# Retention layer on one Trainium2 core: gate projections of two heads in one product, chunk products in three fp32r passes, one state update in eight left out

## The chip, the cores and the metric

The kernel runs on one core of a Trainium2 chip. The metric is the device time of one execution in microseconds (us), taken as the median of several. A core has a matrix engine (TensorE, PE in the profile, with its weight loads as PEld), a vector engine (VectorE, DVE), a scalar engine (ScalarE, ACT), GpSimd (POOL) and a sync engine (SyncE, SP) that here only waits and issues transfers (SPq rows). Each engine runs its own instruction list in order; they meet only in semaphores.

## The reference, cut to what matters

The whole program is a retention layer, a latent attention layer and a gated linear attention layer with its MLP, on 1024 tokens of width 1024. Only the retention layer is changed. It computes, for 8 heads with 128-wide queries and keys, 256-wide values and a 256-wide gate:

```python
proj = rmsnorm(x, g_pre) @ w_in                      # 1024 x 6144
q, k, v, gate = split(proj)                          # per head 128, 128, 256, 256
q = rope(q);  k = rope(k) * RET_QK_DIM ** -0.5
# per head, with a state R (128 x 256) carried over chunks of tokens
o = (q @ k.T * decay) @ v + (q @ R) * xi
R = R * g_c + (k * zeta).T @ v
o = groupnorm(o) * gn_gain
y = (silu(gate) * o) @ w_out
x = x + rmsnorm(y, g_post)
```

The kernel takes chunks of 128 tokens. The state after a head's last chunk is read by nothing.

## The kernel before, in words

**Precision.** The large products are done in fp32r, a format in which a product is one pass of the array. A matrix is split into an upper part (a rounded copy, made by ACT) and a lower part (the rest, made by DVE), and a product is three passes: lower by upper, upper by lower, upper by upper. The small products of a chunk (scores, scores by values, queries by state, keys by values) are plain fp32, which the trace shows as two records for each matmul.

**Loops.** The retention stage is 64 steps: head h = 0 to 7 outside, token tile t = 0 to 7 (128 tokens) inside, s = 8h + t. The first head and the last are written out, the ones between stand in a loop. A head's weights (8 row tiles kt of 128 x 768: q, k, v and gate columns) are loaded with 768 KB for two row tiles, then split by `w_upper` (ACT) and `w_lower` (DVE), one row tile in each step of the head before. There are two slots for split weights (`inh`, `inl`) and two for raw ones (`inraw`).

**One step on each engine**, in program order:
- PE (`step`): `project` of tile s into q, k, v (24 matmuls of 512 columns); the two transposes of q and k of s-1; `attend(s-2)` (the products `ra_o_ps` by scores, `ra_o_ps` by state, `ra_k_ps`); `project` of the gate of s (24 of 256 columns); `scores(s-1)`.
- ACT: `w_upper` of the next head; copy of the transposed q, k of s-1; copy of q, k, v of s out of PSUM; copy of the output of s-2; `silu` of the gate of s.
- DVE: `w_lower`; `norm_and_gate(s-3)`, which gives the finished tile and counts `G_done`; `carry_state(s-2)`; `moments(s-2)`; `decay_scores(s-1)`, which gives `sT` and counts `sT_done`.
- POOL: rotation of q, k of s (six operations), the decayed keys `kz`, then `deviation(s-2)`.
- SP (`head`): for even t, `load_raw` of row tiles t and t+1 of the next head; then `store(s-3)`, which waits for `G_done` of s-3 and issues the store of the gated tile to DRAM. Whatever stands behind this wait is issued only after it.

**After the last head** the gated tiles come back from DRAM, are transposed, and are multiplied by the 16 row tiles of `w_out` (512 KB each, split by `row_upper` on ACT and `row_lower` on DVE, through raw places given by `row_place`). The first three row tiles are split inside the retention block, and PE does the first four half-products (`multiply`) between the last two `attend`.

Of the kernel before, what the change touches and what calls it, by code (L numbers as in the profile page):

```python
# [17 lines left out]
F32 = mybir.dt.float32  # L18
# [70 lines left out]
def retention_columns(w):  # L89

    w = w.reshape(KT, P, -1)
    parts = [w[:, :, 0:DM].reshape(KT, P, RET_HEADS, RQK), w[:, :, DM:2 * DM].reshape(KT, P, RET_HEADS, RQK),
             w[:, :, 2 * DM:2 * DM + RET_W].reshape(KT, P, RET_HEADS, RV),
             w[:, :, 2 * DM + RET_W:].reshape(KT, P, RET_HEADS, RV)]
    return np.ascontiguousarray(np.concatenate(parts, axis=3).transpose(2, 1, 0, 3))
# [63 lines left out]
def retention_and_latents(nc, place, x, x_cols, gain_in, w_in, gated, w, gain, g_post, x_next, g_kv, g_pre, w_lat, w_gate, g_lat,  # L159
# [8 lines left out]
    with ExitStack() as ctx:  # L168
# [10 lines left out]
        WC = QKV + RV  # L179
        tokh = place("ra_xh", [P, KT, SEQ], F32R, 0)  # L180
        tokl = place("ra_xl", [P, KT, SEQ], F32R, 32 * KB)
        inh = place("ra_wh", [P, 2, KT, WC], F32R, 64 * KB)
        opening = place("ra_opening", [P, 2 * KT * WC], F32, 112 * KB)
        inl = place("ra_wl", [P, 2, KT, WC], F32R, 112 * KB)
        inraw = place("ra_raw", [P, 2, 2, WC], F32, 160 * KB)
        rcos = place("ra_cos", [P, NT, RQK // 2], F32, 172 * KB)
        rsin = place("ra_sin", [P, NT, RQK // 2], F32, 174 * KB)
        decay = place("ra_decay", [P, RET_HEADS, P], F32, 176 * KB)
        qkv = place("ra_qkv", [P, 2, QKV], F32, 180 * KB)
        rot = place("ra_rot", [P, 2, 2, RQK], F32, 184 * KB)  # L190
        rtmp = place("ra_rtmp", [P, 2, RQK], F32, 186 * KB)
        kz = place("ra_kz", [P, 2, RQK], F32, 187 * KB)
        qkT = place("ra_qkT", [P, 2, 2, P], F32, 188 * KB)
        sT = place("ra_sT", [P, P], F32, 190 * KB)
        R = place("ra_R", [P, RV], F32, 190 * KB + 512)
        sg = place("ra_sg", [P, 4, RV], F32, 191 * KB + 512)
        oS = place("ra_oS", [P, 2, RV], F32, 195 * KB + 512)
        SMALL = 197 * KB + 512
# [9 lines left out]
        def cols(t):  # L208

            return staging[:, t % 2, :].rearrange("p (k n) -> p k n", k=KT)  # L210

        def rows(t):

            at = 2 * KT * WC - (2 - t % 2) * DM
            return opening[:, at:at + DM]

        def first_raw(kt):

            return inraw[:, kt // 2, kt % 2, :] if kt < 4 else opening[:, (KT + kt - 4) * WC:(KT + kt - 3) * WC]
# [7 lines left out]
        ROW_AT = [80] + [8 * i for i in range(8)] + [88, 96, 136, 144, 152, 104, 168]  # L227
# [7 lines left out]
        row3 = place("wa_row3", [P, DM], F32, 168 * KB)  # L235
# [7 lines left out]
        LH_FREE, LL_FREE, XH_FREE, XL_FREE = 4, 7, (9, 11), (12, 14)  # L243
# [21 lines left out]
        with ExitStack() as second:  # L265
# [11 lines left out]
        first_in = [sem(f"ra_first_in{i}") for i in range(4)]  # L277
        inraw_in = [sem("ra_raw_in0"), sem("ra_raw_in1")]
        g_out = [sem(f"ra_g_out{i}") for i in range(4)]
        (xss_done, xrms_part, xrms_done, tokh_done, tokl_done, inh_done, inl_done, qkv_mm, qkv_copied,  # L280
         rot_part, rot_done, kz_done, qkT_mm, qkT_copied, s_mm, sT_done, attend_mm, R_done, o_copied, gate_mm,
         silu_done, bn_part, mv_done, rstd_part, rstd_done, norm_part, G_done) = (sem("ra_" + n) for n in (
            "ss_done xrms_part xrms_done tokh_done tokl_done inh_done inl_done qkv_mm qkv_copied "
            "rot_part rot_done kz_done qkT_mm qkT_copied s_mm sT_done attend_mm R_done o_copied gate_mm "
            "silu_done bn_part mv_done rstd_part rstd_done norm_part G_done").split())
        LAST = RET_HEADS * NT
        N_CON = 6
# [4 lines left out]
        row3_in = sem("wa_row3_in")  # L292
# [19 lines left out]
        gin1 = xin[:, :, :].rearrange("p a n -> p (a n)")[:, 0:KW * P].rearrange("p (k n) -> p k n", n=P)  # L312
        EARLY_A = {1: (0, 0), 2: (0, 1), 3: (0, 2), 5: (0, 3), 6: (1, 1), 7: (1, 3)}
        EARLY_B = {5: (1, 0), 6: (1, 2)}
# [5 lines left out]
        def row_place(kt):  # L320

            if kt == 3:
                return row3[:, :], row3_in, 16
            if kt in (6, 7, 10, 11, 14, 15):
                return y[:, kt % 2, :], y_row_in[kt % 2], 16 * ((kt - 2) // 4)
            if kt < 2:
                return staging[:, kt, :], w_arrived[kt], 16
            slot, nth = {2: (0, 2), 4: (1, 2), 5: (0, 3), 8: (1, 3), 9: (0, 4), 12: (1, 4), 13: (0, 5)}[kt]
            return staging[:, slot, :], w_arrived[slot], 16 * nth
# [33 lines left out]
        def _(sp):  # L363
            def load_cols(t):
                if t >= 2:
                    sp.wait_ge(tokl_done, t - 1)
                sp.dma_start(staging[:, t % 2, :], x_cols[t, :, :]).then_inc(cols_in[t % 2], 16)

            def load_rows(t):
                if t >= 2:  # L370
                    sp.wait_ge(xss_done, t - 1)
                sp.dma_start(rows(t), x[t * P:(t + 1) * P, :]).then_inc(rows_in[t % 2], 16)

            def load_first(kt):
                to = (KT + kt - 4) * WC
                dst = inraw[:, kt // 2, :, :] if kt < 4 else opening[:, to:to + 2 * WC].rearrange("p (k n) -> p k n", k=2)
                sp.dma_start(dst, w_in[0, :, kt:kt + 2, :]).then_inc(first_in[kt // 2], 16)

            def load_raw(h, kt):
                slot = kt // 2 % 2  # L380
                sp.dma_start(inraw[:, slot, :, :], w_in[ds(h, 1), :, kt:kt + 2, :].rearrange("a p k n -> p (a k) n"))\
                  .then_inc(inraw_in[slot], 16)
# [3041 lines left out]
```

## Time and profile before

| | us |
|---|---|
| median of 3 runs | 2610.97 (2609.92 to 2613.78) |
| the profiled execution | 2608.52 |
| its span in the trace | 2606.7 |
| PE busy | 2556.7 (98%) |
| DVE busy | 1146.5 (44%) |
| ACT busy | 864.9 (33%) |
| POOL busy | 418.7 (16%) |

Read it so: PE is busy nearly all the time over the whole program, so what counts is how much PE work there is and where PE waits. The retention stage lies from 0 to about 666 us; the rest is the same in both kernels. Busy time of matmuls overlaps (they are pipelined), so the cost of one is read from the distance between the starts of two, not from its duration.

### The profile page before, as it was taken

Reading aid. Unit: us, or ns where it says so; the run is one execution under the profiler, and the core shown is the slowest. Engines: PE = TensorE matmul, PEld = TensorE weight load, DVE = VectorE, ACT = ScalarE, POOL = GpSimd, SP = SyncE. Lnnn points to the kernel's source line nnn. Section 1 sums busy time; section 2 is a strip of 40 time slices with the busy share of each in tenths; the row PEclk is TensorE's granted clock in tenths of the full one; section 3 lists DMA queues with packets and bytes.
Section 4 is the critical chain, followed back from the end, with each engine's and each line's share of the span. In section 5 each row is a group of like instructions: output and inputs, shape, how many; then the busy total and the mean of one; then the engine's idle time right before and its main releaser. Section 6 shows DMA issues by size and latency. Waiting matters only on the chain.

```text
span 2606.7 us, 35858 instructions
## 1 busy us (share of the span) xinstructions
PE 2556.7 (98%) x13176; PEld 2180.0 (84%) x13176; DVE 1146.5 (44%) x2235; ACT 864.9 (33%) x1584; POOL 418.7 (16%) x892
## 2 busy tenths in 40 slices
PE   8999999999999999999999999999999999999999
PEld 7888888888887987788878888888888888888887
DVE  4333333322512521477765777666343343334334
ACT  5322222222312422555444545343331122112212
POOL 4443434343100312200001011101000000000000
PEclk9999999999999999999999999999999999999999
DMA  6211111120523322121243111122331120112111
GB/s 238 76 50 50 48 61 49 50 73 27 202 73 111 98 77 71 30 59 58 70 156 130 60 44 44 46 67 94 126 130 49 49 64 32 48 48 64 32 49 73
DMA packets 71877, 194.21 MB, mean 75 GB/s; under 512 B 8160, under 2 KB 28000, under 8 KB 71008
## 3 DMA queue, kind: packets, MB, share of 16 engines
q1 hardware_dynamic: 71776, 192.85, 22.5%
q8 instruction: 65, 1.06, 0.2%
q14 instruction: 36, 0.29, 0.0%
HBM read 152.45 MB, written 36.18 MB: 72 GB/s over the span
## 4 chain that ended last, share of the span: by engine, by line
PE 53%; DVE 4%; issue 2%; ACT 2%; DMA 0%; ACTq 0%; DVEq 0%; POOL 0%; POOLq 0%
PE wc_g_ps L3197 13%; PE wc_y_ps L3213 13%; PE gl_vr_ps L2334 7%; PE gl_j_ps L2293 3%; PE wb_y_ps L2664 3%; PE wc_y_ps L2946 3%; PE gl_l_ps L2360 2%; DVE at_nmax L1577 1%; PE at_v_ps L1652 1%; DVE gate_lower L1584 1%; PE at_v_ps L1653 1%; PE at_v_ps L1654 1%; PE at_j_ps L1652 1%; PE gl_o_ps L2345 1%; PE gl_k_ps L2348 1%
## 5 line engine op out<-in xcount | busy, mean ns | idle before, releaser
L1068 PE MATMUL ra_qkv_ps<-ra_wh,ra_xl 128*128 (+1 forms) x512 | 207.0, 404 | 11.5 <-DVE ra_wl L903 9.2
L1068 PE MATMUL ra_qkv_ps<-ra_wh,ra_xh 128*128 (+1 forms) x512 | 201.3, 393 | 0.0
L1068 PE MATMUL ra_qkv_ps<-ra_wl,ra_xh 128*128 (+1 forms) x512 | 200.8, 392 | 0.0
L3197 PE MATMUL wc_g_ps<-x_upper,ff_w1l 128*128 128x512 f32 x512 | 199.3, 389 | 0.0
L3197 PE MATMUL wc_g_ps<-x_upper,ff_w1h 128*128 128x512 f32 x512 | 199.2, 389 | 0.0
L3213 PE MATMUL wc_y_ps<-ff_w2h,ff_hl 128*128 128x512 f32 x512 | 199.2, 389 | 0.0
L3213 PE MATMUL wc_y_ps<-ff_w2l,ff_hh 128*128 128x512 f32 x512 | 199.2, 389 | 0.0
L3197 PE MATMUL wc_g_ps<-x_lower,ff_w1h 128*128 128x512 f32 x512 | 199.2, 389 | 0.0
L3213 PE MATMUL wc_y_ps<-ff_w2h,ff_hh 128*128 128x512 f32 x512 | 199.2, 389 | 0.0
L3151 DVE TENSOR_TENSOR ff_acc<-wc_y_ps,ff_acc 128x1024 f32<-128x1024 f32 x63 | 77.1, 1225 | 210.9 <-PE wc_y_ps L3213 210.9
L3076 ACT ACTIVATE ff_relu<-wc_g_ps 128x512 f32<-128x512 f32 x64 | 38.3, 598 | 378.1 <-PE wc_g_ps L3197 378.1
L1068 PE MATMUL ra_gate_ps<-ra_wh,ra_xl 128*128 (+1 forms) x512 | 155.7, 304 | 0.0
L1068 PE MATMUL ra_gate_ps<-ra_wh,ra_xh 128*128 (+1 forms) x512 | 144.7, 283 | 0.0
L1068 PE MATMUL ra_gate_ps<-ra_wl,ra_xh 128*128 (+1 forms) x512 | 144.6, 282 | 0.0
L3137 DVE SCALAR_TENSOR_TENSOR wc_g_ps<-wc_g_ps,ff_relu 128x512 f32<-128x512 f32 x64 | 44.8, 700 | 178.8 <-ACT ff_relu L3076 178.8
L1068 PEld LDWEIGHTS ra_qkv_ps<-ra_wh,ra_xl 128*128 128x128 f32 x512 | 97.1, 190 | 30.0 <-issue 11.7
L570 ACT ACTIVATE ra_qkT<-ra_T_ps 128x256 f32<-128x256 f32 x63 | 24.1, 383 | 282.1 <-PE ra_T_ps L1078 282.1
L1068 PEld LDWEIGHTS ra_qkv_ps<-ra_wh,ra_xh 128*128 128x128 f32 x512 | 97.0, 189 | 21.4
L3213 PEld LDWEIGHTS wc_y_ps<-ff_w2l,ff_hh 128*128 128x128 f32 x512 | 96.1, 188 | 19.9
L3213 PEld LDWEIGHTS wc_y_ps<-ff_w2h,ff_hl 128*128 128x128 f32 x512 | 96.1, 188 | 19.9
L3197 PEld LDWEIGHTS wc_g_ps<-x_lower,ff_w1h 128*128 128x128 f32 x512 | 96.1, 188 | 19.9
L3197 PEld LDWEIGHTS wc_g_ps<-x_upper,ff_w1h 128*128 128x128 f32 x512 | 96.1, 188 | 19.9
(409 smaller groups left out, 6442.4 us busy)
## 6 DMA issues: line engine op xcount, KB each, us to landing
staging<-in_w_ff SPq DMA_DIRECT2D x64, 512.0 KB, 3.8
ra_raw<-in_w_in_a SPq DMA_DIRECT2D x30, 768.0 KB, 4.6
gated_a<-ra_sg SPq DMA_DIRECT2D x64, 128.0 KB, 1.9
staging<-in_w_vr_c SPq DMA_DIRECT2D x16, 512.0 KB, 4.2
wa_gin<-gated_a SPq DMA_DIRECT2D x6, 1024.0 KB, 4.9
staging<-in_w_out_a SPq DMA_DIRECT2D x9, 512.0 KB, 4.1
staging<-in_x_cols SPq DMA_DIRECT2D x8, 512.0 KB, 5.1
ra_opening<-in_x SPq DMA_DIRECT2D x8, 512.0 KB, 7.6
```

Source lines behind the costliest of these rows:

```text
L1068: last = pe.matmul(out, a[:, kt, t * P:(t + 1) * P], b[:, ds(slot, 1), kt, at:at + n].rearrange("p a n -> p (a n)"), start=(kt == 0 and i ...
L1652: pe.matmul(out, al, bh, start=start, stop=False)
L2293: last = pe.matmul(out, w[:, r, cols], xx[:, r, at], start=(r == 0 and i == 0), stop=(r == KT - 1 and i == 2))
L2334: last = pe.matmul(vr_ps[t % 2][:, :], xx[:, r, t * P:(t + 1) * P], w[:, r, :], start=(r == 0 and i == 0), stop=(r == KT - 1 and i == 2))
L2360: last = pe.matmul(l_ps[:, level * (P // 2):(level + 1) * (P // 2)].rearrange("p (g n) -> p g n", n=n), lv_main[c][:, level, at], lv_main[ ...
L2664: last = pe.matmul(y_ps[t % 2][:, c, :], a[t % 2][:, kt, :], b[kt][:, c * HALF:(c + 1) * HALF], start=(kt == 0 and i == 0), stop=(kt == KW ...
L2946: last = pe.matmul(y_ps[t % 2][:, c, :], a[t % 2][:, kt, :], b[kt][:, c * HALF:(c + 1) * HALF], start=(kt == 0 and i == 0), stop=(kt == KW ...
L3076: act.activation(relu[:, :], f_ps[j % 2][:, :], ACT.Relu).then_inc(relu_done, 1)
L3137: dve.scalar_tensor_tensor(f_ps[j % 2][:, :], f_ps[j % 2][:, :], 0.0, relu[:, :], ALU.max, ALU.mult).then_inc(sq_done, 1)
L3151: dve.tensor_tensor(acc[t][:, :], y_ps[t % 2][:, :, :].rearrange("p a n -> p (a n)"), acc[t][:, :], ALU.add).then_inc(y_added, 1)
L3197: last = pe.matmul(f_ps[j % 2][:, :], a[kt // 2][:, kt % 2, f * P:(f + 1) * P], b[:, kt, half * HALF:(half + 1) * HALF], start=(kt == 0 an ...
L3213: last = pe.matmul(y_ps[t % 2][:, n, :], a[:, f, t * P:(t + 1) * P], b[f][:, n * HALF:(n + 1) * HALF], start=(f == 0 and i == 0), stop=(f ...
```

## The change

- `retention_columns` now lays the weights out as a wide array for each pair of heads (q, k, v of the even head, the gates of both heads: 1024 columns) and a narrow one (q, k, v of the odd head: 512 columns). PE's gate product is done in the even head alone, 512 columns wide, for both; `silu` writes the odd head's half into `kept`, which lies in `staging`.
- There is one slot each for wide and narrow split weights. The next pair's wide weights are loaded one row tile (512 KB) in each step of the odd head and split there (`wide_upper`, `wide_lower`); the narrow ones two row tiles (512 KB) in every other step of the even head.
- The three chunk products run in three fp32r passes (`three`). So the scores, the transposed queries, the state, the decayed keys and the values are split: upper parts by ACT (the keys' by POOL's own product), lower parts by DVE (`scores_lower`, `queries_lower`, `state_lower`, `keys_lower`, `values_lower`).
- `scores` moves from the end of step s+1 to the middle of `project` in step s+2, two steps behind.
- For t = 7 the product `ra_k_ps` and the state update are left out.
- The first row tiles of `w_out` go other ways: 0, 1, 3, 4 through `inraw`; 2 and 5 through `staging`, which holds `kept` until the last tiles are stored; row 5 is loaded only after the last store has landed. Four row tiles are split inside the block.

```diff
-            def head(h, first, more):
+            def load_wide(pair, kt):
+                sp.wait_ge(inl_done, splits(pair, kt - 2))
+                sp.dma_start(inraw[:, kt % 2, :], w_wide[ds(pair, 1), :, kt, :].rearrange("a p n -> p (a n)"))\
+                  .then_inc(inraw_in[kt % 2], 16)
...
+            def odd_head(pair):
+                h = 2 * pair + 1
                 for t in range(NT):
-                    if more and t % 2 == 0:
-                        sp.wait_ge(inl_done, t + 2 if first and t < 4 else KT * h + KT + t - 2)
-                        load_raw(h + 1, t)
...
+                    load_wide(pair + 1, t)
+                    if t == 3:
+                        sp.wait_ge(sT_part, NT * h)
+                        load_decay(h + 1, 0)
+                    store_third_last(h, True, t)
+
+            def even_head(pair):
+                h = 2 * pair
+                for t in range(NT):
+                    if t % 2 == 0:
+                        load_narrow(pair, t // 2)
+                    if t == 3:
+                        sp.wait_ge(sT_part, NT * h)
+                        load_decay(h + 1, 1)
+                    store_third_last(h, False, t)
```

ACT, first for the order in a step, then for the first head and the odd heads:

```diff
+            def step(s, h, t, older, middle=lambda: None):
+
+                if older >= 2:
+                    scores_upper(s - 2)
+                middle()
+                act.wait_ge(qkv_mm, s + 1)
+                if older < 4:
+                    act.wait_ge(xrms_done, t + 1)
+                act.activation(qk[:, t % 2, :], qkv_ps[t % 2][:, 0:2 * RQK], ACT.Copy, scale=xrms[:, 1, t:t + 1]).then_inc(qkv_copied, 1)
                 if older >= 1:
+                    transposed(s - 1, (t - 1) % NT)
                 if older >= 2:
                     act.wait_ge(attend_mm, s - 1)
+                act.activation(vh[:, t % 2, :], qkv_ps[t % 2][:, 2 * RQK:QKV], ACT.Copy, scale=xrms[:, 1, t:t + 1]).then_inc(vh_done, 1)
                 if older >= 2:
+                    output(s - 2, h if t >= 2 else h - 1, (t - 2) % NT, older >= 4)
...
             for t in range(NT):
-                step(t, 0, t, t)
-                silu(t, 0, t, t)
+                if t == NT - 2:
+                    act.wait_ge(tokl_done, NT)
+                if t >= NT - 2:
+                    for i in (2 * t - 2 * NT + 4, 2 * t - 2 * NT + 5):
+                        narrow_upper(0, i)
+                step(t, 0, t, min(t, 3))
+                silu(0, t, True)
                 if t + 2 < NT:
                     square_x(t + 2)
                     x_upper(t + 2)
-                w_upper(1, 1, t)
...
+            def odd_head(pair):
+                h = 2 * pair + 1
                 for t in range(NT):
+                    if t == 0:
+                        act.wait_ge(gate_mm, NT * pair + NT)
+                    wide_upper(pair + 1, t)
                     step(h * NT + t, h, t, 4)
```

DVE:

```diff
+            def step(s, pair, odd, t, older, middle=lambda: None):
...
+                if older >= 2:
+                    decay_scores(s - 2, *head_of(2), (t - 2) % NT)
+                if older >= 1:
+                    keys_lower(number(1), (t - 1) % NT)
+                if older >= 2:
+                    scores_lower(s - 2)
+                middle()
+                if older >= 3:
+                    norm_and_gate(s - 3, *head_of(3), (t - 3) % NT)
+                if older >= 1:
+                    queries_lower(s - 1, (t - 1) % NT)
+                if older >= 2:
+                    carry_state(s - 2, number(2), (t - 2) % NT)
+                values_lower(s, t)
+                if older >= 2:
+                    moments(s - 2, (t - 2) % NT)
+                    state_lower(number(2), (t - 2) % NT)
...
+            def odd_head(pair):
                 for t in range(NT):
+                    wide_lower(pair + 1, t)
+                    step((2 * pair + 1) * NT + t, pair, True, t, 3)
```

PE:

```diff
+            def three(out, high, low, start, stop):
+
+                (ah, bh), (al, bl) = high, low
+                pe.matmul(out, al, bh, start=start, stop=False)
+                pe.matmul(out, ah, bl, start=False, stop=False)
+                return pe.matmul(out, ah, bh, start=False, stop=stop)
...
+            def step(s, h, t, weights, older, pair=None, between=lambda: None, middle=lambda: None):
                 if older >= 2:
+                    pe.wait_ge(vl_done, s - 1)
+                out, as_they_come = qkv_ps[t % 2][:, :], None if older else 0
+                project(out, t, weights, 0, range(KT // 2), as_they_come)
+                if older >= 2:
+                    scores(s - 2)
+                middle()
+                project(out, t, weights, 0, range(KT // 2, KT), as_they_come).then_inc(qkv_mm, 1)
                 if older >= 1:
                     transpose_qk(s - 1, (t - 1) % NT, older >= 2)
                 if older >= 2:
+                    attend(s - 2, h if t >= 2 else h - 1, (t - 2) % NT, older >= 3)
                 between()
+                if pair is not None:
+                    if older:
+                        pe.wait_ge(silu_done, NT * pair + t)
+                    project(gate_ps[:, :], t, weights, QKV, range(KT), None if older else KT).then_inc(gate_mm, 1)
```

## Rows read from the trace of the kernel before

**Rows 1.** The waits of PE, 0 to 900 us: total, times, longest.

```profile
PE ra_qkv_ps L1068 <- DVE ra_wl L903: 9.2, 1, 9.2
...
PE ra_qkv_ps L1068 <- DVE ra_wl L864: 2.4, 1, 2.4
PE wa_y_ps L346 <- DVE wa_wl L339: 1.7, 1, 1.7
```

**Rows 2.** Timeline of PE over one step: start us, us, engine, line, operands, count.

```profile
299.73 0.47 PE L1068 MATMUL ra_gate_ps<-ra_wh,ra_xl 128*128 x1
...
300.15 0.28 PE L1068 MATMUL ra_gate_ps<-ra_wh,ra_xh 128*128 x1
...
302.78 0.39 PE L1098 MATMUL ra_s_ps<-ra_qkT 128*128 128x128 f32 x2
...
303.70 0.40 PE L1068 MATMUL ra_qkv_ps<-ra_wh,ra_xl 128*128 x1
...
308.25 0.39 PE L1068 MATMUL ra_qkv_ps<-ra_wh,ra_xh 128*128 x1
308.49 0.38 PE L1078 MATMUL ra_T_ps<-ident,ra_rot 128*128 128x128 f32 x2
308.70 0.60 PE L1089 MATMUL ra_o_ps<-ra_qkv,ra_sT 128*128 128x256 f32 x2
309.14 0.59 PE L1091 MATMUL ra_o_ps<-ra_R,ra_qkT 128*128 128x256 f32 x2
309.57 0.59 PE L1092 MATMUL ra_k_ps<-ra_qkv,ra_kz 128*128 128x256 f32 x2
309.81 0.47 PE L1068 MATMUL ra_gate_ps<-ra_wh,ra_xl 128*128 x1
```

**Rows 3.** Timeline around a store and a load, DVE and SP queue, same columns.

```profile
105.95 0.43 DVE L876 TENSOR_TENSOR ra_sg<-ra_oS,ra_sg 128x256 f32<-128x256 f32 x1
...
106.55 0.34 SPq L387 DMA_DIRECT2D gated_a<-ra_sg  x1
...
107.14 0.36 SPq L381 DMA_DIRECT2D ra_raw<-in_w_in_a  x1
```

**Rows 4.** DMA issues of 100 to 600 us: KB each, median us from issue to landing.

```profile
ra_raw<-in_w_in_a SPq DMA_DIRECT2D x23, 768.0 KB, 4.5
gated_a<-ra_sg SPq DMA_DIRECT2D x50, 128.0 KB, 1.9
```

**Rows 5.** DMA issues of 1900 to 2600 us, the same columns.

```profile
staging<-in_w_ff SPq DMA_DIRECT2D x60, 512.0 KB, 3.7
```

**Rows 6.** Groups of ACT, 0 to 700 us: busy us, mean ns of one, idle before.

```profile
L588 ACT ACTIVATE ra_sg<-ra_gate_ps,ra_rx 128x256 f32<-128x256 f32 x64 | 30.4, 475 | 109.9 <-PE ra_gate_ps L1068 109.9
...
L570 ACT ACTIVATE ra_qkT<-ra_T_ps 128x256 f32<-128x256 f32 x63 | 24.1, 383 | 282.1 <-PE ra_T_ps L1078 282.1
L335 ACT ACTIVATE wa_wh<-staging,gains 128x1024 fp32r<-128x1024 f32 x9 | 10.3, 1147 | 9.6 <-DMA staging<-in_w_out_a 9.5
```

**Rows 7.** Groups of DVE, 0 to 700 us, the same columns.

```profile
L876 DVE TENSOR_TENSOR ra_sg<-ra_oS,ra_sg 128x256 f32<-128x256 f32 x64 | 27.2, 426 | 2.2
...
L872 DVE TENSOR_SCALAR ra_oS<-ra_oS,ra_mv,ra_rstd 128x256 f32<-128x256 f32 x64 | 26.3, 411 | 28.8 <-POOL ra_rstd L784 28.8
L898 DVE TENSOR_TENSOR ra_sT<-ra_s_ps,ra_decay 128x128 f32<-128x128 f32 x64 | 18.7, 291 | 77.0 <-PE ra_s_ps L1098 77.0
...
L339 DVE SCALAR_TENSOR_TENSOR wa_wl<-staging,gains,wa_wh 128x1024 fp32r<-128x1024 f32 x9 | 11.5, 1284 | 9.4 <-ACT wa_wh L335 9.4
```

**Rows 8.** Timeline of PE from its wait at 88 us.

```profile
90.75 0.54 PE L1068 MATMUL ra_qkv_ps<-ra_wh,ra_xl 128*128 x1 [2.37 <-DVE ra_wl L864]
...
94.50 0.39 PE L1068 MATMUL ra_qkv_ps<-ra_wh,ra_xl 128*128 x1
```

**Rows 9.** Timeline of the SP queue at the end of the stage.

```profile
670.09 0.34 SPq L387 DMA_DIRECT2D gated_a<-ra_sg  x1
...
674.15 0.33 SPq L461 DMA_DIRECT2D wa_gin<-gated_a  x1
```

More of the change, by code:

```diff
@@ L91, in retention_columns @@
     w = w.reshape(KT, P, -1)
[L92 to L95, printed above, removed]
+    qk = [w[:, :, i * DM:(i + 1) * DM].reshape(KT, P, RET_HEADS, RQK) for i in range(2)]
+    v, gate = (w[:, :, 2 * DM + i * RET_W:2 * DM + (i + 1) * RET_W].reshape(KT, P, RET_HEADS, RV) for i in range(2))
+    own = np.concatenate(qk + [v], axis=3)
+    wide = np.concatenate([own[:, :, 0::2], gate[:, :, 0::2], gate[:, :, 1::2]], axis=3)
+    lay = lambda part: np.ascontiguousarray(part.transpose(2, 1, 0, 3))
+    return lay(wide), lay(own[:, :, 1::2])
 def wait_alone(eng):
@@ L208, in cols, with first_raw, gated_tile, states @@
         def cols(t):
[L210 to L219, printed above, removed]
+            src = staging if t < 2 else late_cols
+            return src[:, t % 2, :].rearrange("p (k n) -> p k n", k=KT)
+        def first_raw(kt, half):
+            return first_raws[kt // 2][:, kt % 2, half * HALF:(half + 1) * HALF]
+        def gated_tile(odd, t):
+            return kept[:, t, :] if odd else sg[:, t % 4, :]
+        def states(h, t):
+            return (NT - 1) * h + t
+        WIDES, NARROWS = KT, KT // 2
+        PIECES = WIDES + NARROWS
+        def splits(pair, j):
+            return PIECES * pair + KT + j + 1
         KW = RET_W // P
@@ L565, in step, with first_upper, wide_upper @@
-            def step(s, h, t, older):
-                hp = h if t >= 2 else h - 1
+            def first_upper(kt, half):
+                act.wait_ge(first_in[half][kt // 2], 16)
+                act.activation(wide[0][:, kt, half * HALF:(half + 1) * HALF], first_raw(kt, half), ACT.Copy,
+                               scale=gain_in[:, kt:kt + 1]).then_inc(inh_done, 1)
+            def wide_upper(pair, kt):
+                act.wait_ge(inraw_in[kt % 2], 16 * (PIECES // 2 * pair + kt // 2 - KT // 2 + 1))
+                act.activation(wide[0][:, kt, :], inraw[:, kt % 2, :], ACT.Copy, scale=gain_in[:, kt:kt + 1]).then_inc(inh_done, 1)
@@ new lines, in narrow_upper, with scores_upper @@
+            def narrow_upper(pair, i):
+                act.wait_ge(inraw_in[i % 2], 16 * (PIECES // 2 * pair + i // 2 + 1))
+                for kt in (2 * i, 2 * i + 1):
+                    last = act.activation(narrow[0][:, kt, :], inraw[:, i % 2, kt % 2 * NARROW:(kt % 2 + 1) * NARROW],
+                                          ACT.Copy, scale=gain_in[:, kt:kt + 1])
+                last.then_inc(inh_done, 1)
+            def scores_upper(s):
+                act.wait_ge(sT_part, s + 1)
+                act.activation(sTh[:, :], sT[:, :], ACT.Copy).then_inc(sTh_done, 1)
@@ L1120, in _ @@
                     pe.wait_ge(ident_in, 16)
[L1121 removed]
+                step(t, 0, t, wide, t, 0)
             def transpose_first(tile, q):
```

528 lines of the change are left out of this document (298 added, 230 removed).

## The prediction

> **What bounds the kernel now.** I read the waits of PE first [rows 1]: over the whole retention stage PE waits 9.2 us at the start, 2.4 us once, and 1.7 us once in the product that follows. Between these it never waits for another engine, so the stage is the sum of its matmuls. The timeline of one step gives their prices [rows 2]. A step, from gate product to gate product, is 309.81 - 299.73 = 10.08 us. A 512-column pass takes (308.25 - 303.70)/20 = 0.2275 us, a 256-column pass (302.78 - 300.15)/22 = 0.1195 us. The three fp32 products start 0.44 and 0.43 us apart, and I take 0.43 for the third. So PE has no slack, and every other engine has. The question is what slack is left when a step of PE gets short. For that I read the queue around a store and a load [rows 3], what a load takes to land [rows 4, 5], and what an element-wise operation costs on ACT and DVE [rows 6, 7].
>
> **Part 1: gates of two heads in one product.** Before, two heads pay 48 x 0.1195 = 5.74 us for a tile's gates, after 24 x 0.2275 = 5.46 us [rows 2]: 0.28 us saved, 32 times, **-9.0 us**.
>
> **Part 2: three passes.** 3 x 0.1195 = 0.36 us in place of 0.43 to 0.44 [rows 2]. Scores by values 64 x 0.08 = 5.1, queries by state 56 x 0.07 = 3.9, keys by values 56 x 0.07 = 3.9 us: **-12.9 us**. That a pass keeps its 0.1195 us here is taken from the gate's passes; the other bound is a rival below.
>
> **Part 3: last state.** 8 x 0.43 = **-3.4 us** [rows 2].
>
> **Part 4: the new step lengths.** An even head's step becomes 10.08 - 2.87 + 5.46 - 0.22 = 12.45 us, an odd head's 10.08 - 2.87 - 0.22 = **6.99 us**. The parts add up to the same: 12.45 + 6.99 is 0.72 us under 2 x 10.08.
>
> **Part 5: what the short step uncovers.** In heads 1, 3 and 5 the wide weights are fetched and split, one row tile a step. SP's list is: load of row tile t, then the store of tile s-3, which waits for `G_done` of s-3; only then comes the load of t+1. But ACT wants t+1 ahead of everything else in step s+1, DVE splits it ahead of `decay_scores(s-1)`, and `norm_and_gate(s-2)`, which gives the next `G_done`, stands behind that on DVE. So there is a ring that goes round once a step, and the load is inside it:
>
> - end of the gating product to the issue of the load: 107.14 - 106.38 = 0.76 us [rows 3] (the store's own issue lies between);
> - issue to landing of 512 KB: 3.7 us, the median of 60 loads of this size [rows 5]. From the 128 and 768 KB of this stage, 1.9 and 4.5 us, a straight line gives 3.46 [rows 4]; 4.5 is the upper bound;
> - `wide_upper`, 128x1024: 1.15 us [rows 6];
> - handing on to another engine: 0.17 us (DVE's end at 106.38 to SP's issue at 106.55 [rows 3]);
> - `wide_lower`, 128x1024: 1.28 us [rows 7];
> - `decay_scores`: 0.29 us, with its start 0.32 [rows 7];
> - handing on, `scores_upper`: 0.17 + 0.28 us. No copy of 128x128 is in the trace; it lies between nothing and the 0.38 us of 256 columns [rows 6], and I take it near the upper end;
> - handing on, `scores_lower`: 0.17 + 0.27 us, just under the 0.29 of its neighbour [rows 7];
> - `norm_and_gate`: 0.41 + 0.43 us with starts, 0.90 [rows 7].
>
> The sum is **9.17 us** against 6.99 us of PE work. PE stands in this ring too: `attend(s-2)` waits for `sT_done`, so behind it `project` of the next step waits. Each round costs 2.18 us. Step 0 of an odd head is free of it, since its row tile was loaded during the long even step. In step 1 the load is issued 6.7 us after the last gate product and the scores are ready at 14.3, where PE would come at 12.9: 1.4 us. Steps 2 to 7 cost 6 x 2.18 = 13.1 us. Step 0 of the next even head meets the narrow load in the same ring. Its two 512-column splits take 1.28 us on ACT and 1.42 us on DVE (between the 256- and 1024-column prices of rows 6 and 7), so 9.44 - 6.99 = 2.45 us. Together 17.0 us for a pair, three times: **+51 us**. In the other even steps the same ring has 12.45 us and is hidden. In head 7 nothing wide is loaded. There the early work on `w_out` is two row tiles that came long before; the chain from `attend` through copy, split and scores ends about 0.4 us before PE needs it, so I cost it at nothing.
>
> The Trainium skill ("DMA: Bandwidth & Descriptors", section on the anatomy of one DMA) fits a transfer as about 2.0 us plus its bytes at 436 GB/s, which is an estimate of 3.2 us for 512 KB, for a path other than SP's. By it the forecast would be some 11 us lower; the measured 3.7 us is used. Its constant part alone would leave the ring longer than PE's step, so this rule speaks against the change as well.
>
> **Part 6: head 0.** Before, PE waited 2.37 us when head 1's last split came late, and then ran at half clock: nine passes in 94.50 - 90.75 = 3.75 us instead of 2.05 [rows 8]. After, the narrow weights are ready before the last gate product ends: **-4.1 us**. What takes its place is in step 6. ACT does `silu` twice (0.95 us [rows 6]), squares and copies the last tile (two of 128x1024, 2.3 us), then waits for `x_lower` (1.28 us on DVE) before the first `narrow_upper`, because these weights lie on the column buffer. Then come four copies of 512 columns (2.56), the last pair's split (1.42) and the scores' chain (1.21, from the ring). Counted from `attend` with PE's 6.54 us to the end of its gate product that is 17.0 us against 12.45: 4.6 us late. Step 7 is 0.6 us late, steps 2 to 5 0.2 us each: **+6 us**. In the opening, DVE's half pieces of 512 columns let PE start about 1 us sooner, and the first gate product then waits for eight more pieces. I take no change, within 2 us either way.
>
> **Part 7: the end of the stage.** Before, PE lost 1.7 us there [rows 1]. After, I follow the lists from the last `attend` but two. The state split of tile 62 stands ahead of the last scores on DVE: 1.0 us. `row_lower(2)` comes behind the last scores: 0.6. `row_lower(3)` and `row_lower(4)` stand behind the last two tiles' normalisation, which takes DVE, POOL and DVE in turn: 1.3 us each. Row tile 5 can be asked for only when the last store has landed (1.9 us, median [rows 4]; here before 4.06 us lay between that issue and the next block's first load, with other loads under way [rows 9]). It then needs 3.7 + 1.15 + 0.17 + 1.28 us while PE has one row tile of 2.7 us left: 4.8 us late, and then likely half clock, 1.7 us. Together 10.7, less the old 1.7: **+9 us**.
>
> **Part 8: clock.** A wait of 1.7 us [rows 1] left the passes behind it at full rate, one of 2.37 us halved it [rows 8]. In the odd steps a half-rate spell of 3.75 us costs 1.7 us and still fits in the 2.18 us that PE would wait. The four waits that stand before long steps (head 0, three even heads) do not have that cover: half of 4 x 1.7 us, **+3.4 us**.
>
> **Sum.** -9.0 - 12.9 - 3.4 - 4.1 = -29.4; +51 + 6 + 9 + 3.4 = +69.4; net **+40 us**. The profiled execution took 2608.5 us, so 2648.5; it lies 2.5 us under the median of the runs, so **2651 us**.
>
> **Rivals.**
>
> *The loads stay hidden (faster).* The ring closes before PE comes, and only parts 6 and 7 are paid: -29.4 + 15 = -14 us, 2597 us. For: both kernels have 16 DMA engines that are mostly idle here, and the loads before waited for nothing that PE saw in the loop. Against: the ring would have to be under about 7.6 us for the result to turn faster, which is a landing of about 2.1 us. Only the 128 KB stores land so fast [rows 4]. Or my order of the lists would have to be wrong. Chance 0.09, with a further 0.03 for a ring close to that point and no change, 2609 us.
>
> *Half clock in every odd step.* If the clock, once down, stays down between the waits, an odd step is 6.99 x 0.43/0.2275 = 13.1 us, above the ring: 21 x 3.9 = +83 us, 2734 us. For: the 2.37 us wait was enough for a fall, and these are of that size. Against: nine passes brought it back [rows 8]. The Trainium skill ("TensorE: Matmul & The Clock Gate", section on oscillation) describes a kernel that fell to half clock at each wait for a load. Chance 0.05.
>
> *Three passes cost more than one fp32 product*, because nine weight loads stand where six did. At 0.19 us for a pass in place of 0.1195 the 40 steps that PE sets would be 0.63 us longer each: +25 us, 2676 us. Against: the gate's passes change weights each time at 0.1195 [rows 2]. Chance 0.05.
>
> **Chances and range.** My forecast has 0.78. Its own range: landing at 3.46 us takes 5 us off, at 4.5 us adds 19; the copy of the scores -3 or +2; parts 6 and 7 at half, -7.5; clock and opening 4 either way. That is 2632 to 2675 us. To hold eight in ten it goes to 2624 and to 2680, which takes in the weight-load case. Within 0.2% (5 us, about what a measurement of this kernel can tell from no change): 0.03. Faster 0.09, slower 0.88.
>
> **What the profile after would show.** PE waits on DVE's `ra_sTl`, about 24 times, near 50 us in total, in heads 1, 3 and 5 and the first step after each; ACT's `ra_wide_h` waits for the load of `ra_raw` in those steps; steps of 9.2 us there, 12.4 us in even heads, 7.0 us in head 7; starts of the chunk products 0.36 us apart; loads of 512 KB landing in 3.5 to 4 us. A PE wait behind the third row tile of `w_out` and one of about 5 us at row tile 5. I am wrong if odd steps are near 7 us, if the passes are further apart than 0.12 us, or if the clock in heads 1, 3 and 5 is far under 1.

## The result, and the profile after

The changed kernel takes **2650.35 us** (median of 4 runs, 2649.15 to 2652.44) where the kernel before takes 2610.78 us (4 runs, 2609.92 to 2613.78). The ratio is **1.0151**, with a 95% interval of 1.0136 to 1.0166: slower by 39.6 us. The forecast was 2651 us, with a range of 2624 to 2680.

The head of the page after: span, busy time of each engine, and the tenths of PE and of its clock in 40 slices.

```profile
span 2647.3 us, 35102 instructions
...
PE 2552.5 (96%) x12568; PEld 2142.4 (81%) x12568; DVE 1231.7 (47%) x2540; ACT 919.9 (35%) x1840; POOL 398.1 (15%) x884
...
PE   8989899899999999999989999999999999999999
...
PEclk9999999999999999999999999999999999999999
```

PE has become less busy (96% where it was 98%), and four of the five slices with an 8 lie in the first fifth of the span: the loss is in the retention stage and is idle time. What PE waits for from 0 to 900 us (total, times, longest), the counterpart of [rows 1]:

```profile
PE ra_o_ps L1257 <- DVE ra_sTl L1032: 36.5, 22, 3.2
PE ra_qkv_ps L1242 <- DVE ra_wide_l L973: 8.5, 1, 8.5
PE wa_y_ps L372 <- DVE wa_wl L365: 5.3, 3, 3.9
...
PE ra_qkv_ps L1242 <- issue: 3.9, 2, 2.2
```

The first row is new, and it is the one the forecast named. It says only who came last, though: DVE's lower part of the scores. To see why that is late one goes a step back, to what ACT waits for (same window, same columns):

```profile
ACT ra_wide_h L628 <- DMA ra_raw<-in_w_wide_a: 61.5, 21, 4.5
ACT ra_narrow_h L633 <- DMA ra_raw<-in_w_narrow_a: 8.1, 3, 2.8
```

21 waits for the wide load and 3 for the narrow one behind it: the 24 places of part 5. The loads themselves are not slow; DMA issues of 100 to 600 us (KB each, median us to landing), the counterpart of [rows 4, 5]:

```profile
ra_raw<-in_w_wide_a SPq DMA_DIRECT2D x24, 512.0 KB, 3.9
ra_raw<-in_w_narrow_a SPq DMA_DIRECT2D x12, 512.0 KB, 3.6
gated_a<-staging SPq DMA_DIRECT2D x24, 128.0 KB, 2.1
```

One full turn of the ring, from the timeline of all engines (start us, duration us, engine, line, operands; in brackets the idle time before and who ended it):

```profile
346.79 0.39 PE L1257 MATMUL ra_o_ps<-ra_vh,ra_sTl 128*128 128x256 f32 x1 [1.89 <-DVE ra_sTl L1032]
...
347.18 0.48 DVE L996 TENSOR_TENSOR staging<-ra_oS,staging 128x256 f32<-128x256 f32 x1
...
347.83 0.35 SPq L421 DMA_DIRECT2D gated_a<-staging  x1
...
348.43 0.33 SPq L406 DMA_DIRECT2D ra_raw<-in_w_wide_a  x1
...
348.85 0.63 PE L1242 MATMUL ra_qkv_ps<-ra_narrow_h,ra_xh 128*128 128x512 f32 x1
...
352.13 1.15 ACT L628 ACTIVATE ra_wide_h<-ra_raw,gains 128x1024 fp32r<-128x1024 f32 x1 [2.75 <-DMA ra_raw<-in_w_wide_a]
...
353.31 1.29 DVE L978 SCALAR_TENSOR_TENSOR ra_wide_l<-ra_raw,gains,ra_wide_h 128x1024 fp32r<-128x1024 f32 x1 [3.15 <-ACT ra_wide_h L628]
...
354.51 0.28 DVE L1028 TENSOR_TENSOR ra_sT<-ra_s_ps,ra_decay 128x128 f32<-128x128 f32 x1
354.83 0.31 ACT L639 ACTIVATE ra_sTh<-ra_sT 128x128 fp32r<-128x128 f32 x1 [1.55 <-DVE ra_sT L1028]
...
355.18 0.29 DVE L1032 TENSOR_TENSOR ra_sTl<-ra_sT,ra_sTh 128x128 fp32r<-128x128 f32 x1
355.39 0.41 DVE L992 TENSOR_SCALAR ra_oS<-ra_oS,ra_mv,ra_rstd 128x256 f32<-128x256 f32 x1
...
355.53 0.39 PE L1257 MATMUL ra_o_ps<-ra_vh,ra_sTl 128*128 128x256 f32 x1
...
355.92 0.42 DVE L996 TENSOR_TENSOR staging<-ra_oS,staging 128x256 f32<-128x256 f32 x1
```

Read downwards from 347.18 and leave the PE lines out: each line waits for one above it. They are the gating product, store issue, load issue, 3.70 us to ACT's copy, the two halves of the split, the scores with their two halves, normalisation, and the next gating product 8.74 us after the first. PE's products at 346.79 and 355.53 hang on this ring at the lower part of the scores, although PE has only 7.04 us of work in a step. The first waited 1.89 us for it. The second shows no wait of its own, since PE's granted clock was 0.50 from 348.0 to 351.2 us (passes 0.43 us apart, as at 348.85), which filled the time that it would have waited; it starts 0.06 us after the lower part ends, as the first does.

### The profile page after: what moved, and what is told of

Same layout as the page of the kernel before. It is cut to its first block, busy times and chain, and to the rows that moved or that the text cites. A ratio compares the mean times of both kernels' runs of the same rounds, so it can differ in the third digit from the quotient of the medians.

```text
span 2647.3 us, 35102 instructions
## 1 busy us (share of the span) xinstructions
PE 2552.5 (96%) x12568; PEld 2142.4 (81%) x12568; DVE 1231.7 (47%) x2540; ACT 919.9 (35%) x1840; POOL 398.1 (15%) x884
## 4 chain that ended last, share of the span: by engine, by line
PE 52%; DVE 4%; issue 2%; ACT 2%; DMA 0%; ACTq 0%; DVEq 0%; POOL 0%; POOLq 0%; SPq 0%
PE wc_g_ps L3396 13%; PE wc_y_ps L3412 13%; PE gl_vr_ps L2533 7%; PE wb_y_ps L2863 3%; PE wc_y_ps L3145 3%; PE gl_j_ps L2492 2%; PE gl_l_ps L2559 2%; DVE at_nmax L1776 1%; PE at_v_ps L1851 1%; PE at_v_ps L1853 1%; PE at_v_ps L1852 1%; DVE gate_lower L1783 1%; PE gl_o_ps L2544 1%; PE at_j_ps L1851 1%; PE gl_k_ps L2547 1%
## 5 line engine op out<-in xcount | busy, mean ns | idle before, releaser
L3396 PEld LDWEIGHTS wc_g_ps<-x_upper,ff_w1l 128*128 128x128 f32 x512 | 96.1, 188 | 19.9
L3412 PEld LDWEIGHTS wc_y_ps<-ff_w2h,ff_hh 128*128 128x128 f32 x512 | 96.1, 188 | 19.9
L1242 PE MATMUL ra_qkv_ps<-ra_wide_h,ra_xl 128*128 128x512 f32 x256 | 104.0, 406 | 8.5 <-DVE ra_wide_l L973 8.5
L372 PE MATMUL wa_y_ps<-wa_wh,wa_gl 128*128 128x512 f32 x256 | 103.7, 405 | 6.1 <-DVE wa_wl L365 5.3
L1242 PE MATMUL ra_qkv_ps<-ra_narrow_h,ra_xl 128*128 128x512 f32 x256 | 106.0, 414 | 0.0
L1242 PE MATMUL ra_qkv_ps<-ra_narrow_h,ra_xh 128*128 128x512 f32 x256 | 102.1, 399 | 3.9 <-issue 3.9
L1242 PE MATMUL ra_qkv_ps<-ra_narrow_l,ra_xh 128*128 128x512 f32 x256 | 102.1, 399 | 0.0
L2533 PE MATMUL gl_vr_ps<-gl_vrh,x_lower 128*128 128x512 f32 x256 | 101.8, 398 | 0.3 <-DVE gl_vrl L2301 0.3
```

The costliest lines, as they stand in the source:

```text
L372: last = pe.matmul(y_ps[slot][:, c, :], a[:, slot, kt, :], b[kt][:, c * HALF:(c + 1) * HALF], start=(kt == 0 and i == 0), stop=(kt == KW - ...
L1242: last = pe.matmul(out, a[:, kt, t * P:(t + 1) * P], b[:, kt, at:at + HALF], start=(kt == 0 and i == 0), stop=(kt == KT - 1 and i == 2))
L2533: last = pe.matmul(vr_ps[t % 2][:, :], xx[:, r, t * P:(t + 1) * P], w[:, r, :], start=(r == 0 and i == 0), stop=(r == KT - 1 and i == 2))
L3396: last = pe.matmul(f_ps[j % 2][:, :], a[kt // 2][:, kt % 2, f * P:(f + 1) * P], b[:, kt, half * HALF:(half + 1) * HALF], start=(kt == 0 an ...
L3412: last = pe.matmul(y_ps[t % 2][:, n, :], a[:, f, t * P:(t + 1) * P], b[f][:, n * HALF:(n + 1) * HALF], start=(f == 0 and i == 0), stop=(f ...
```

## Experiments

Eleven kernels ran. Each was measured beside the kernel before, whose median was 2610.3 to 2611.0 us in all three groups. Where there are intervals, a kernel was timed in several rounds; the others have one execution and are read by their trace.

**e1_load_ahead**: in odd heads SP issues the load of a row tile one place earlier, before the store that it stood behind, and the first narrow load of the next even head likewise.

```diff
+                load_wide(pair + 1, 0)
                 for t in range(NT):
-                    load_wide(pair + 1, t)
+                    if t + 1 < NT:
+                        load_wide(pair + 1, t + 1)
+                    else:
+                        load_narrow(pair + 1, 0)
...
                     store_third_last(h, True, t)
```

> The changed kernel with one thing moved on SP: in an odd head the load of row tile t+1 is issued ahead of the store of tile s-3 and no longer behind it (and the first narrow load of the next head ahead of the last store). Nothing else differs. Theory (a ring through SP's wait for the finished tile, with the load inside it): the load gains a whole step, the ring of 8.8 to 9.0 us may then take two steps, and the odd steps fall to PE's own 7.0 to 7.2 us; the waits of PE for the lower scores, 36.5 us in the changed kernel, fall under 5; the time falls by about 45 us, to 2605 us (2600 to 2612). First rival (the added copies and differences on ACT and DVE fill the short step by themselves): the odd steps stay above 8.5 us and the time stays within 10 us of 2650. Second rival (a halved clock makes the odd steps long): the waits go but the steps stay above 8 us with a low granted clock.

Measured: **2608.89 us**, ratio 0.9991 (0.9981 to 1.0), so 41.5 us less than the changed kernel. Its PE waits, 0 to 900 us:

```profile
PE wa_y_ps L372 <- DVE wa_wl L365: 5.7, 3, 4.3
...
PE ra_qkv_ps L1246 <- issue: 5.3, 4, 2.5
PE ra_o_ps L1261 <- DVE ra_sTl L1036: 3.2, 1, 3.2
```

22 waits on the scores became one (that of head 0), and the odd steps take 6.68 to 7.05 us. The element-wise work is the same; only the place of one DMA issue moved. The ring stood on that place.

**e2_half_load**: the wide loads of heads 2 to 7 bring only the first half of each row (the gate columns keep what stood in the buffer before).

```diff
-  sp.dma_start(inraw[:, kt % 2, :], w_wide[ds(pair, 1), :, kt, :]...
+  sp.dma_start(inraw[:, kt % 2, 0:HALF], w_wide[ds(pair, 1), :, kt, 0:HALF]...
```

> The changed kernel with the wide loads of the later pairs cut to their first 512 columns, 256 KB; the queue order stays and the splits keep their full size. It leaves out the load of the gate columns of heads 2 to 7. Theory (ring with the load inside): a straight line through 128 KB at 2.0 and 512 KB at 3.9 us gives 2.65 us, so the ring shortens by about 1.2 us, from 8.8 to about 7.6; PE waits about 0.5 us in a step in place of 1.7; the time falls by about 25 us, to 2625 us. Rival (the splits and the new operations, not the load, set the step): no change, 2650 us.

Measured: 2632.86 us. A load of 256 KB lands in 2.9 us where 512 KB took 3.9 (DMA issues, 100 to 600 us), and the waits on the scores fall from 36.5 to 22.9 us:

```profile
ra_raw<-in_w_wide_a SPq DMA_DIRECT2D x24, 256.0 KB, 2.9
```

From the issue of a wide load to the start of ACT's split it is 3.10 us on average over the 21 turns in the ring, where the changed kernel has 4.06, and a turn takes 8.14 us where it took 9.11. So 0.96 us less of landing took 0.97 us out of each turn, and 17.5 us off the whole. That is what a ring with the landing inside it does. The whole time is 8 us above the expectation: this load was put at 2.65 us, and eight of the 21 needed 3.3 to 3.9.

**e3_split_behind_scores**: loads as in the changed kernel, but ACT and DVE do the scores of a step first and the split behind them.

```diff
-                    wide_upper(pair + 1, t)
-                    step(h * NT + t, h, t, 4)
+                    step(h * NT + t, h, t, 4, lambda: wide_upper(pair + 1, t))
```

> The changed kernel with the wide splits moved in ACT's and DVE's order from ahead of the scores of s-2 to behind them (still ahead of the normalisation of s-3); SP's order stays. Theory (ring through the load and the finished tile): the scores leave the ring, but the split and the normalisation stay in it: 0.76 + 3.7 + 1.15 + 1.3 + 0.95 = 7.9 us a round, so odd steps of about 7.9 to 8.1 us, and the time falls by 16 to 20 us, to about 2632 us. Rival (the split standing ahead of the scores is the whole cause, and the late load is harmless): the scores come in time in every step, odd steps of 7.0 to 7.2 us, and the time falls by 45 us to 2605 us.

Measured: 2635.51 us, with odd steps of 7.9 to 8.3 us. The waits, 0 to 900 us:

```profile
PE ra_o_ps L1255 <- DVE ra_sTl L1031: 15.4, 17, 3.3
PE ra_qkv_ps L1240 <- DVE ra_wide_l L977: 8.5, 3, 2.9
```

A turn takes 8.15 us on average. The scores' chain left the ring and the load stayed in it, so the ring is shorter but there. The gain, 14.8 us, is a little under the 16 to 20 expected. The second row shows what that costs elsewhere: the last split of a head now comes late for the next even head's first product, up to 2.9 us.

**e4_row5** and **e5_head0** each mend one of the smaller places of the changed kernel. In e4 row tile 5 of `w_out` goes to the buffer of the gates, which head 7 does not use, so that it is asked for before the last stores have landed; in e5 ACT and DVE split head 1's narrow columns of head 0's last two steps behind the scores, the ones off the column buffer first.

```diff
+            if kt == 5:
+                return sg[:, :, :].rearrange("p a n -> p (a n)"), row5_in, 16
...
-                    for i in (2 * t - 2 * NT + 4, 2 * t - 2 * NT + 5):
-                        narrow_upper(0, i)
-                step(t, 0, t, min(t, 3))
...
+                    for j in (2 * t - 2 * NT + 4, 2 * t - 2 * NT + 5):
+                        narrow_upper(0, j, (j + 2) % 4)
+                step(t, 0, t, min(t, 3), split if t >= NT - 2 else lambda: None)
```

> The changed kernel with row tile 5 of the output weights loaded to the place of the even heads' gates, which is free in the last head, and not behind the last store. Nothing else differs. Theory: the wait of 3.86 us at row tile 5 and the 1.7 to 1.9 us at half clock behind it go, the two waits of 0.7 us stay: 5 to 6 us less, about 2644.5 us. Rival (DVE is late there anyway, because of the last two tiles' normalisation): the wait only shrinks to 1 to 2 us and the gain stays under 3 us.

> The changed kernel with the narrow splits of head 0 moved in steps 6 and 7 from ahead of the scores to behind them on ACT and DVE, row tiles 4 to 7 first (they do not lie on the column buffer, so ACT need not wait for the last lower part of x). Nothing else differs. Theory (part 6: the splits stand in the chain to the scores): the wait of 3.25 us at step 6 goes and with it the half clock behind it; from the product of tile 3's scores to that of tile 6's the time falls from 43.8 us to 3 x 12.5 = 37.5 us. The whole falls by about 6 us, but a single time can hide it, so the distance in the timeline decides. Rival (the last lower part of x comes late in any case): a wait of 1 us or more stays in step 6 or 7.

Both waits as they stand in the changed kernel: the first is row tile 5's, the second the one behind `x_lower` in head 0. Each is gone in the kernel that mends it.

```profile
712.63 0.50 PE L372 MATMUL wa_y_ps<-wa_wh,wa_gl 128*128 128x512 f32 x1 [3.86 <-DVE wa_wl L365]
```

```profile
87.75 2.56 ACT L633 ACTIVATE ra_narrow_h<-ra_raw,gains 128x512 fp32r<-128x512 f32 x4 [1.29 <-DVE ra_xl L967]
...
92.78 0.58 PE L1257 MATMUL ra_o_ps<-ra_vh,ra_sTl 128*128 128x256 f32 x1 [3.25 <-DVE ra_sTl L1032]
```

e4 took 2647.0 us. From the last chunk product of the stage to the first transpose that waits for its block it is 49.1 us, against 54.8 in the changed kernel: 5.7 us as expected, of which its whole time shows 3.4, since the stage ahead of it was longer in this execution (39.0 us of waits on the scores). e5 took 2642.7 us: three steps of head 0 need 37.44 us, the plain 3 x 12.48, where they needed 43.82. Its whole time shows 7.7 us, in a single execution.

**e6_ahead_plain** and **e10_ahead_plain_unrolled** price the three passes: e1 with one fp32 product of the upper parts in their place (the lower parts are left out of the chunk products), with TensorE's loop and with the loop written out. **e7_ahead_unrolled** is e1 with the loop written out and the three passes kept.

```diff
-                pe.matmul(out, al, bh, start=start, stop=False)
-                pe.matmul(out, ah, bl, start=False, stop=False)
-                return pe.matmul(out, ah, bh, start=False, stop=stop)
+                return pe.matmul(out, ah.bitcast(F32), bh.bitcast(F32), start=start, stop=stop)
```

```diff
-            with pe.Fori(0, RET_HEADS // 2 - 1) as pair:
+            for pair in range(RET_HEADS // 2 - 1):
```

> e1_load_ahead with each chunk product done as one plain fp32 product of the upper parts in place of three fp32r passes; the lower parts are still computed by DVE and waited for. It leaves out the lower parts from these products. This prices part 2 by itself. Theory (0.43 us against 0.36 us, 64 + 56 + 56 products, PE sets every step): +0.07 us x 176 = +12 us against e1_load_ahead, so about 2621 us, starts of the chunk products 0.43 us apart, odd steps 7.25 us. Rival (three passes cost as much as a plain product, because of nine weight loads where six stood): within 4 us of e1_load_ahead, 2609 us.

> e1_load_ahead with PE's loop over the three pairs written out; the other engines keep their loops. In the changed kernel and in e1_load_ahead PE stands 2 to 3 us for no engine or transfer at both turns of this loop, and the clock then falls. Theory (the turn of the long loop costs PE the fetch of its next instructions): both waits go and the half clock behind them, 4 to 8 us less than e1_load_ahead, about 2603 us. Rival (the wait belongs to something else that comes at these places, such as a transfer that takes the instruction fetch's place, and a straight program has to be fetched as well): the same waits stand at the same steps, or others at other places, and the time stays within 2 us of 2609.

> Loads one place ahead, one plain fp32 product in place of the three fp32r passes (it leaves out the lower parts in the chunk products), and TensorE's loop written out, beside the same kernel with three passes at 2595.4. Theory (three passes take 0.21 us less per step over 59 steps without other waits, and what hid this in the looped pair of runs was the turn of the loop): 2595.4 + 12.4 = 2607.8, range 2605 to 2611. Rival (three passes cost as much as the plain product because they draw the clock down): the two within 3 us of each other, 2593 to 2598.

Measured: e6 2610.38 us (ratio 1.0, 0.9991 to 1.001), e7 **2595.4** (0.9939, 0.9922 to 0.9955), e10 2610.1 (0.9996, 0.9986 to 1.0006). By e6 alone, only 1.5 us over e1, the three passes looked nearly worthless, although its steps were longer as expected (7.25 and 12.70 us where e1 has 7.04 and 12.48). The gap was in e1, not in e6: e1 has 5.3 us of waits named issue, e6 has none. e7, too, gained more than the 4 to 8 us expected of it: 13.5. With the loop written out on both sides the passes are worth 2610.1 - 2595.4 = **14.7 us**. In the two traces 12.2 of these lie in the retention stage (its last chunk product starts at 657.82 and 645.65 us), near the 12.9 of part 2; the rest lies behind it, in code that is the same in both. The rival in which the passes cost more than a product has fallen.

**e9_unrolled_only** and **e8b_all_loop** price the loop itself: e9 is the changed kernel with the loop written out; **e8_all** has every mend (loads ahead, splits behind the scores, e4, e5, no loop), e8b the same with the loop.

> The changed kernel with the three turns of TensorE's loop over pairs of heads written out; the other engines' programs are as in the changed kernel. Theory (a turn of this long loop costs TensorE a wait called issue of 1.7 to 2.2 us, and in some turns a stretch of half clock behind it): the two issue waits of 3.9 us in all and the 0.7 to 0.8 us by which the turns exceed them go, 2650.4 - 4.7 = 2645.7 at least; if the clock also holds where it fell behind them, down to 2640. Rival (the written-out kernel with the early loads won its 13.5 us because it had no other waits, and the turns are hidden here behind the 3.2 us waits of the odd steps): 2650 within 1.

> All of it together: the load ahead of the store, the wide splits behind the scores, row tile 5 to a place of its own, the narrow splits of head 0 behind the scores, PE's loop over pairs written out. By the theories of the single runs, from the 2609 us of e1_load_ahead: row tile 5 -6, head 0 -6, the loop's turns -4 to -8, and the wide splits behind the scores nothing, since that chain is hidden once the load is early: 2590 to 2595 us, 0.6 to 0.8% under the kernel before. Rival for the last item: if the splits behind the scores hold up the normalisation, waits for the lower scores or the wide weights appear in heads 1, 3, 5 and it stays above 2600 us.

> All mends (loads ahead, splits behind the scores, row tile 5 read earlier, narrow columns of head 0 split later) with TensorE's loop kept, beside the same with the loop written out at 2583.7. Theory (the loop's turns cost 13 us together with the clock behind them, as they did between the two kernels with early loads alone): 2597, range 2592 to 2600. Rival (most of the 13.5 us between those two was chance of the clock in single executions, the turns being worth the 5.3 us of their issue waits): 2589, range 2587 to 2591.

Measured: e9 2643.52 us (ratio 1.0122, 1.0105 to 1.0139), 6.8 under the changed kernel; e8b 2596.08 (0.9944, 0.9928 to 0.9961); e8 **2583.73** (0.9895, 0.9878 to 0.9911), 12.3 under e8b and 6 under what was expected, since the loop was priced there at 4 to 8 us. All that is left to PE's waits in e8, 0 to 900 us:

```profile
PE ra_qkv_ps L1249 <- DVE ra_wide_l L980: 8.1, 1, 8.1
PE wa_T_ps L1367 <- DMA wa_gin<-gated_a: 3.7, 2, 3.4
PE wa_y_ps L375 <- DVE wa_wl L368: 1.5, 2, 0.7
PE wa_y_ps L375 <- DVE ra_vl L1056: 0.6, 1, 0.6
```

A turn of the loop in e8b, from PE's timeline:

```profile
262.25 0.39 PE L1249 MATMUL ra_gate_ps<-ra_wide_h,ra_xh 128*128 128x512 f32 x1
262.89 0.49 PE L1249 MATMUL ra_qkv_ps<-ra_narrow_h,ra_xl 128*128 128x512 f32 x1 [0.26 <-issue]
263.23 0.39 PE L1249 MATMUL ra_qkv_ps<-ra_narrow_l,ra_xh 128*128 128x512 f32 x1
266.11 0.50 PE L1249 MATMUL ra_qkv_ps<-ra_narrow_h,ra_xh 128*128 128x512 f32 x1 [2.49 <-issue]
...
267.68 0.63 PE L1249 MATMUL ra_qkv_ps<-ra_narrow_l,ra_xh 128*128 128x512 f32 x1
268.11 0.63 PE L1249 MATMUL ra_qkv_ps<-ra_narrow_h,ra_xh 128*128 128x512 f32 x1
...
271.26 0.39 PE L1249 MATMUL ra_qkv_ps<-ra_narrow_l,ra_xh 128*128 128x512 f32 x1
271.48 0.39 PE L1249 MATMUL ra_qkv_ps<-ra_narrow_h,ra_xh 128*128 128x512 f32 x1
```

PE issues two passes of the odd head's first product, stands for 2.49 us with no engine to wait for, and soon runs for 3 us with its passes 0.43 us apart in place of 0.23. The step around it takes 17.39 us in place of 12.48; the other turn costs 3.23. e8 has neither. These are 8.1 of the 12.3 us; nearly all of the rest lies behind the stage, in code that neither touches.

What is brought in at a turn can be read in the rows of the DMA queues, in those that the profile calls instruction (packets, MB, share of 16 engines). From 250 to 450 us, e1 with the loop and e7 with it written out:

```profile
q8 instruction: 13, 0.21, 0.5%
```

```profile
q8 instruction: 8, 0.13, 0.3%
```

In the same stretch neither e6 nor the kernel before has such a row: their last transfer of this kind in the loop starts at 243.7 and 153.2 us. So the body of e1 and e8b is brought in again at each round, the shorter ones are not. In e8b one of these transfers starts at 260.2 and one at 263.3 us, around the wait that ends at 266.11. In e7 and e8 they come one by one, and PE stands for none of them.

## Why the prediction was right

The number came out within 1 us, and the mechanism is the one forecast. Some of its terms erred against each other.

- **Parts 1 to 4, right.** Steps are 12.48 and 7.04 us, forecast 12.45 and 6.99. A pair of heads without waits takes 154.72 us (e8, heads 2 and 3) where it took 160.58, so four pairs save 23.4 us, forecast 25.3. The passes of the chunk products start 0.12 us apart.
- **Part 5, the ring: right in its links, with two sizes that erred against each other.** The 21 turns with a wide load took 8.66 to 10.07 us, **9.11 on average**, against 9.17; the turn shown above is one of the shortest. From the gating product to the load's issue it was 0.77 us and in ACT's split 1.15, both as forecast. From the issue to ACT's start it was 3.66 to 5.03 us, 4.06 on average, where 3.7 was taken. From the end of ACT's split to the end of the next gating product it was 3.12 us, where the links add up to 3.56: starts and hand-overs overlap there. Heads 1, 3 and 5 took 70.95, 71.05 and 71.09 us where 55.60 do in e7 and e8: 46.3 us, forecast 51. Over the three heads, the difference is not in steps 2 to 7 (39.0 us for 39.3) but in step 1 (1.5 for 4.2) and in the step with the narrow load (5.7 for 7.4). PE's listed waits there are 33.2 us and not near 50, since 8.5 us of the 46.3 went into half clock, under which PE has less to wait, and a wait is counted only from the end of the matmul before it. With the loop's turns out on both sides, e9 less e7, the ring costs **48.1 us**. That it is the *place* of the load is shown by e1; that the landing is inside, by e2; that the scores' chain is, by e3. The rival of hidden loads has fallen.
- **Part 6, head 0: right place, too dear.** Step 6 was 3.5 us late with a wait of 3.25 (forecast 4.6); steps 2 to 5, put at 0.2 us each, took the plain 12.48 or 12.12. So it was 3.5 us for 6; the half clock behind it is in part 8. The opening came to +0.8 us, within the 2 that were allowed.
- **Part 7, the end: right places, somewhat dear.** Waits of 0.65, 0.72, 0.74 and 3.86 us and about 1.8 of half clock make 7.8 us, forecast 10.7; what e4 took back is 5.7.
- **Part 8, clock: right in size by luck.** Head 0's step after its wait took 15.36 us in place of 12.48: +2.9 us in one place, where 3.4 were forecast for four. The waits before the even heads, 1.5 to 1.7 us, cost nothing: the next steps took 12.48 to 12.50. The rival of half clock in every odd step has fallen: of the 21 waits there, four had a spell of half clock begin at their end or within 1.2 us of it. Those were the waits of 3.13, 2.98 and 2.06 us and one of 1.89 us, the one shown above; one of 2.27 us, the other one of 1.89 and all the shorter ones left the rate. Behind that of 1.89 us the forecast of part 8 can be seen: the step at half clock took 8.74 us, no longer than its ring. The Trainium skill ("TensorE: Matmul & The Clock Gate", section on oscillation) tells of a fall at each wait for a load; this trace agrees only for some of its waits.
- **Not foreseen: the loop's turn.** 15.21 and 14.48 us in place of 12.48 at the two turns, +4.7 us in the profiled execution and 6.8 by e9. It made up for what the ring was overrated by. The end and head 0 were put too dear as well, the gain of parts 1 to 3 too high and the time behind the stage at nothing. So it is luck that the total came within 1 us.

These terms add up to 36.8 us: -23.4 for parts 1 to 3, -4.1 and +0.8 for the old wait and the opening, +6.4 head 0 with its half clock, +46.3 ring, +4.7 turns, +6.1 end. All but the 1.8 of half clock in the end, 35.0 us, lie ahead of row tile 5's first product, which the trace shows 35.9 us later than before (712.63 for 676.76). The last 4.7 us of the 40.6 in the span lie behind it; 1.8 of them are the half clock just named. For the rest no cause was tried; from the stage's last chunk product to the end it is 1940 us in the profiled execution of the kernel before and 1943 to 1955 in those of the others.

What the change is worth without its side effects is the reverse of the verdict: e8 is **1.05% faster** than the kernel before, by 26.5 us, where parts 1, 2, 3 and 6 were forecast to take 29.4 off. Of the three ideas only the passes were priced alone. The change lost because a load kept its place behind a store when the step around it shrank from 10.1 to 7.0 us.

## What to carry to other kernels

When steps get shorter, add up the longest *circle* that goes round once a step through queues and engines, DMA landing and all, and compare it with the new step; an engine at 47% can sit in a circle that sets the pace. A load that must come every step goes ahead of a store that waits for this step's result, and the cure is an order of issues, not a faster operation. Compare two versions of one part only where nothing else waits: e6 against e1 hid a gain of 12 to 15 us behind a loop's turn.

## What the runs showed of the hardware

- **A long loop body on TensorE can cost at its turn.** The loop over pairs, 16 steps, lets PE stand for 1.7 to 2.5 us just after each of its two turns, with no engine waited for, and after three of the six turns of the changed kernel, e1 and e8b some us of half clock followed. The kernel before, with a body of 8 steps, shows no such wait [rows 1]. Nor does e6, whose body is the same but for 44 matmuls and 44 weight loads fewer (one product of two passes for three, 44 times in a pair). Writing it out gave 12.3 to 13.5 us where nothing else waited (8.5 and 10.8 of them in the stage, by the traces), 6.8 us with the ring in place, and 0.3 us with the plain product (e10 against e6). The rows of instruction transfers above fit: only the bodies that stand at their turns are brought in again at each round. No run changed this alone, so that the fetch is what PE waits for is argued from where these transfers lie, not shown.
- **One kernel's runs spread with the clock.** e1 ran from 2603.5 us at a mean granted clock of 0.996 to 2613.5 at 0.991 over 10 runs. e6 and e10 stayed within 3.3 and 4.1 us over 10, e7 and e8, which have the fewest waits, within 1.0 and 0.7 us over 4.
- **Transfers from SP's queue** landed in 2.1 us for 128 KB (stores), 2.9 for 256 and 3.6 to 3.9 for 512 (loads), as medians. Single wide loads of 512 KB in the ring took 3.66 to 5.03 us up to ACT's start, and nearly all of the difference between its turns came from there. The Trainium skill ("DMA: Bandwidth & Descriptors", section on the anatomy of one DMA) has a fit for another path, by which an estimate is 2.6 us for 256 KB, 3.2 for 512 and 2.3 for 128. The landings measured here lie 0.3 to 0.7 us above it for the loads, and 0.2 below it for the store.
